# Six of eight value tiles of the second mixer as Strassen-Winograd pairs, with two weight sums made by adding transfers

## The reference

```python
h = rmsnorm(x, p["mix_norm"][layer])
proj = h @ p["w_in_c"][j]
u = proj[..., :D_C]
v = layernorm(proj[..., D_C:], ...)
z = spatial_gating(v, p["sgu_w"][j], p["sgu_bias"][j])
x = x + (u * z) @ p["w_out_c"][j]
```

## Time and profile before

| | |
|---|---|
| median of 3 runs | 1179.95 us |
| lowest, highest | 1179.23, 1180.22 us |
| span of the profiled execution | 1178.1 us |
| TensorE busy | 1166.1 us |
| last output products, first ConvFFN | 541 to 580 us |
| value units | 580 to 632 us |
| U units, with turning and gating of V | 632 to 705 us |

### The profile page before, as it was taken

How to read it: one execution, slowest core, us unless ns; L and a number is a source line. 1 busy time by engine, 2 the same in 40 slices (tenths; PEclk the granted TensorE clock), 3 DMA queues, 4 the chain that set the end, 5 groups by cost and what they waited for, 6 DMA issues and landing times. The chain is left out here.

```text
span 1178.1 us, 21481 instructions
## 1 busy us (share of the span) xinstructions
PE 1166.1 (99%) x8562; PEld 1146.4 (97%) x8562; DVE 738.1 (63%) x1358; ACT 523.9 (44%) x929; POOL 646.5 (55%) x647
## 2 busy tenths in 40 slices
PE   8999999999999999999999999999999999999997
PEld 8887999999999999999999999999999999999997
DVE  5999766578655786545414644455776557864554
ACT  7465554444344453334412533354443444434452
POOL 3986353448934489343464323345488454884433
PEclk9999999999999999999999999999999999999999
DMA  6310342221422214213322222322124222242212
GB/s 229 115 63 28 76 154 88 71 72 57 145 87 72 71 49 152 87 54 98 119 74 88 68 68 88 110 72 88 55 72 144 72 83 61 72 144 72 67 55 82
DMA packets 33365, 103.74 MB, mean 88 GB/s; under 512 B 4849, under 2 KB 6897, under 8 KB 33265
## 3 DMA queue, kind: packets, MB, share of 16 engines
q1 hardware_dynamic: 29200, 98.92, 25.6%
q10 hardware_dynamic: 4080, 3.69, 1.0%
HBM read 98.29 MB, written 4.79 MB: 87 GB/s over the span
## 5 line engine op out<-in xcount | busy, mean ns | idle before, releaser
L443 PE MATMUL psum<-x_hi,w_hi 128*128 128x288 f32 x1820 | 392.3, 297 | 1.3 <-POOL w_lo L1404 1.3
L443 PE MATMUL psum<-x_hi,w_lo 128*128 128x288 f32 x1820 | 389.8, 296 | 0.0
L443 PE MATMUL psum<-x_lo,w_hi 128*128 128x288 f32 x1820 | 389.7, 296 | 0.0
L1404 POOL TENSOR_TENSOR w_lo<-w_raw,w_hi 128x1024 fp32r<-128x1024 f32 (+2 forms) x100 | 222.5, 2228 | 227.2 <-ACT w_hi L860 227.2
L443 PEld LDWEIGHTS psum<-x_hi,w_hi 128*128 128x128 f32 x1820 | 293.4, 189 | 3.6 <-POOL w_lo L1404 1.6
L443 PEld LDWEIGHTS psum<-x_hi,w_lo 128*128 128x128 f32 x1820 | 293.2, 189 | 0.0
L443 PEld LDWEIGHTS psum<-x_lo,w_hi 128*128 128x128 f32 x1820 | 293.2, 189 | 0.0
L2070 DVE SCALAR_TENSOR_TENSOR psum<-arena,params,psum 128x608 f32<-128x608 f32 x176 | 150.6, 856 | 88.2 <-ACT psum L1205 83.9
L1404 POOL TENSOR_TENSOR w_lo<-arena,w_hi 128x1024 fp32r<-128x1024 f32 (+1 forms) x49 | 114.5, 2337 | 119.5 <-ACT w_hi L860 119.5
L690 PE MATMUL psum<-block_hi,w_hi 128*128 128x288 f32 x448 | 133.6, 298 | 0.0
L690 PE MATMUL psum<-block_hi,w_lo 128*128 128x288 f32 x448 | 133.2, 297 | 0.0
(11 more groups left out here) (232 smaller groups left out, 1666.8 us busy)
## 6 DMA issues: line engine op xcount, KB each, us to landing
w_raw<-in_w_up SPq DMA_DIRECT2D x44, 512.0 KB, 3.3
arena<-in_w_up SPq DMA_DIRECT2D x44, 512.0 KB, 3.2
w_raw<-in_w_down SPq DMA_DIRECT2D x16, 512.0 KB, 3.6
arena<-in_w_down SPq DMA_DIRECT2D x16, 512.0 KB, 3.7
w_raw<-in_w_in_c SPq DMA_DIRECT2D x16, 512.0 KB, 3.2
w_raw<-in_w_in_ab SPq DMA_DIRECT2D x11, 512.0 KB, 3.4
w_raw<-in_w_out_ab SPq DMA_DIRECT2D x16, 256.0 KB, 2.6
w_raw<-in_w_out_c SPq DMA_DIRECT2D x8, 512.0 KB, 3.3
```

What stands on the lines that cost most here:

```text
L443: last = nc.tensor.matmul(PS[:, 2 * (q % 2 if slot is None else slot) + half, 0:HALF], w[q][:, k * P:(k + 1) * P], r[:, r_at, half * HALF: ...
L1404: nc.gpsimd.tensor_tensor(w_lo[slot][:, 0:nk * P], raws[RAW_SLOT[RAW[u]]][:, 0:nk * P], w_hi[slot][:, 0:nk * P].bitcast(F32), ALU.subtract ...
```

## The change

Value tiles 2 to 7 are computed as three pairs. With x cut into two halves of channels and two halves of tokens, and the weights of a pair into two halves of input channels by two output tiles, a pair is a 2x2 product of blocks, and seven products of blocks (4 input tiles x 3 terms = 12 matmuls each) take the place of eight. For this

- VectorE and ScalarE make four sums of blocks of x, split into high and low parts (`x_sums`, `x_sums_hi`), inside the loop over the last output tiles of the first ConvFFN, whose tiles now come in the order 0, 4, 1, 5, 2, 6, 3, 7;
- two of the four sums of weights of a pair (R3, S1) are made by transfers: SP loads A21 twice into a buffer, then a transfer issued by GpSimd adds A11 and A22 to them; VectorE makes the other two (S2, R4);
- each weight block is split on its own (ScalarE, GpSimd, 512 columns), up to eight ahead;
- products accumulate in PSUM on top of copies of earlier ones, which ScalarE makes (`bank_copy`), and VectorE combines the rest on evacuation (`take_c11` to `take_c21`);
- VectorE adds up V in place of GpSimd;
- w_in_c tiles use all four raw buffers; the hidden values of the last group, `xh` and `xl` and two output buffers lie elsewhere, and the scratch for GpSimd's transfers is made smaller to have room.

```diff
+    PAIR_ORDER = ("A11", "S1", "S2", "A12", "R3", "R4", "A22")
+    PAIR_BANK = [{"A11": a, "A12": a, "S1": a + 1, "S2": 0, "R4": 0, "R3": 1, "A22": 1} for a in (2, 6, 2, 6)]
+    PRODUCT_HALF = [(4 + n) % 8 for n in range(N_PRODUCTS - 1)] + [4]
...
+                    raw_tile(m % 4, U_PAIR[m // 2] + (PLACE["A22"] if m % 2 else PLACE["R4"]) + 1)
...
+        X_SUMS_AFTER = (2, 3, 5, 7)
...
+                        if m in (3, 5, 7):
+                            if m > 3:
+                                sp.wait_ge(unit_done, U_IN1)
+                            for n in range(2):
+                                sp.dma_start(dma_sums_of(m // 2)[:, n, :], w_in_c[m, :, 0:KL2]).then_inc(ld_a21[m // 2 - 1], 16)
...
+            unit(0, U_IN1, KD, xh, xl, xl_ready, KD * 2, order=SPLIT_ORDER)
+            def second_norm_sums():
+                pe.wait_ge(xt_ready, 4 * (KD // 2))
+                wide_sums(2)
+
+            unit(1, U_IN1 + 1, KD, xh, xl, middle=second_norm_sums, at_tile=2)
...
+                for n, name in enumerate(PAIR_ORDER):
+                    pe.wait_ge(lo_ready, base + n + 1)
+                    if name == "A11" and p > 1:
+                        pe.wait_ge(acc_free, U_PAIR[p - 2] + 2 if p > 2 else U_IN1 + 2)
+                    elif name == "S2":
+                        pe.wait_ge(pair_copy, copies + 1)
+                    elif name == "R3":
+                        pe.wait_ge(pair_copy, copies + 3)
+                    elif name == "A22":
+                        pe.wait_ge(pair_copy, copies + 4)
...
+            def x_sums_hi(k):
+
+                if k:
+                    act.wait_ge(xt_ready, 4 * k)
+                else:
+                    act.wait_ge(h_lo_ready, H_FFN[0] + NT)
+                nc.scalar.activation(PS[:, M0, 0:HALF], X[:, k, HALF:T], ACT.Identity, bias=0.0,
+                                     scale=pcol("mix_norm", KD + k)).then_inc(xt_hi, 1)
+                for block, bank, sign, made in ((X1, M1, 1.0, 1), (X3, S0, 1.0, 3), (X2, S1, -1.0, 4), (X4, M0, -1.0, 4)):
+                    act.wait_ge(xt_sum, 4 * k + made)
+                    nc.scalar.activation(xth[:, block, k, :], PS[:, bank, 0:HALF], ACT.Copy, scale=sign).then_inc(xt_hi, 1)
...
+            for n in range(1, 4):
+                product_weight_hi(n)
             wide_roots(3)
+            for n in range(4, 8):
+                product_weight_hi(n)
+            for n in range(N_PRODUCTS):
+                if PAIR_ORDER[n % 7] in ("A11", "S1", "S2", "R3"):
+                    bank_copy(n // 7 + 1, PAIR_ORDER[n % 7])
+                if n + 8 < N_PRODUCTS - 1:
+                    product_weight_hi(n + 8)
+                if n == N_PRODUCTS - 5:
+                    product_weight_hi(N_PRODUCTS - 1)
+                    split_n(U_U, U_IN1 + 2 + 14)
+                    split_n(U_U + 1, U_IN1 + 2 + 16)
...
+            def dma_sums(p):
+
+                pool.wait_ge(ld_a21[p - 1], 32)
+                nc.gpsimd.dma_start(dma_sums_of(p), lower_and_upper(p), accum_op=ALU.add).then_inc(dma_sum[p - 1], 16)
+
+            dma_sums(1)
+            for n in range(N_PRODUCTS):
+                product_weight_lo(n)
+                if n in (2, 8):
+                    dma_sums(2 if n == 2 else 3)
...
+            def x_sums(k):
...
+                stt(out=t1, in0=x11, scalar=low, in1=b12, op0=ALU.mult, op1=ALU.subtract).then_inc(xt_sum, 1)
+                stt(out=t3, in0=x22, scalar=high, in1=b12, op0=ALU.mult, op1=ALU.subtract).then_inc(xt_sum, 1)
+                dve.wait_ge(xt_sum, 4 * k + 2)
+                stt(out=t2, in0=x11, scalar=low, in1=t3, op0=ALU.mult, op1=ALU.add).then_inc(xt_sum, 1)
+                dve.wait_ge(xt_sum, 4 * k + 3)
+                stt(out=t4, in0=x21, scalar=high, in1=t2, op0=ALU.mult, op1=ALU.subtract).then_inc(xt_sum, 1)
+                for a, (block, src, sign) in enumerate(((X1, t1, 1.0), (X3, t3, 1.0), (X2, t2, -1.0), (X4, t4, -1.0))):
+                    dve.wait_ge(xt_hi, 5 * k + a + 2)
+                    stt(out=xtl[:, block, k, :], in0=src, scalar=sign, in1=xth[:, block, k, :].bitcast(F32),
+                        op0=ALU.mult, op1=ALU.subtract).then_inc(xt_ready, 1)
...
+            for kind in PAIR_SUMS:
+                pair_weight_sum(1, kind)
             dve.wait_ge(st_ffn, 16)
             wide_factors(3)
-            for m in range(KD):
-                scaled(U_IN1 + m, V[:, m, :])
-            uu = U_IN1 + KD
+            scaled(U_IN1, V[:, 0, :])
+            scaled(U_IN1 + 1, V[:, 1, :])
+            add_v(1)
+            for p in range(1, V_PAIRS):
+                if p < V_PAIRS - 1:
+                    pair_weight_sum(p + 1, "S2")
+                take_c11(p)
+                take_c22(p)
+                if p < V_PAIRS - 1:
+                    pair_weight_sum(p + 1, "R4")
+                take_c12(p)
+                add_v(2 * p)
+                take_c21(p)
+                add_v(2 * p + 1)
...
+    nc = bacc.Bacc("TRN2", target_bir_lowering=False, num_devices=1, dynamic_dma_scratch_size=8192)
```

More of the change, by code:

```diff
@@ L95, in hybrid_trunk @@
     U_IN1 = U_FFN0 + N_FFN
-    U_OUT1 = U_IN1 + 2 * KD
+    V_PAIRS = KD // 2
+    U_PAIR = [None] + [U_IN1 + 2 + 7 * n for n in range(V_PAIRS - 1)]
+    N_PRODUCTS = 7 * (V_PAIRS - 1)
+    U_U = U_IN1 + 2 + N_PRODUCTS + 1
+    U_OUT1 = U_U + KD
     U_FFN1 = U_OUT1 + KD
@@ L135, in hybrid_trunk @@
         IN0[u] = g
-    assert KH == 4 and not any(u % 4 for u in (U_OUT0, U_FFN0, U_IN1, U_OUT1, U_FFN1, *U_GROUP))
+    assert KH == 4 and not any(u % 4 for u in (U_OUT0, U_FFN0, U_IN1, U_OUT1, U_FFN1, U_U, *U_GROUP))
     def tiles_of(u):
@@ L416, in _ @@
                     for m in range(KD):
-                        load(r0 + 2 * n + m, w_down[layer, m, :, t0 * P:(t0 + n) * P])
+                        tile = SPLIT_ORDER[m] if layer == 0 and t0 + n == KF else m
+                        load(r0 + 2 * n + m, w_down[layer, tile, :, t0 * P:(t0 + n) * P])
             for n, r in enumerate(LAST[0][1]):
@@ L1626, in ffn @@
                         continue
-                    for m in range(3, KD + (0 if layer else 3)):
+                    for m in range(3, KD + (0 if layer else 2)):
                         if layer == 0:
@@ L2119, in ffn @@
                         continue
-                    for m in range(KD):
-                        residual(ud + m, m, 2 if m == 2 else None)
-                        x_lo(2, m, "mix_norm", KD + m)
+                    for m, tile in enumerate(SPLIT_ORDER):
+                        residual(ud + m, tile, 2 if m == 2 else None)
+                        x_lo(2, m, "mix_norm", KD + tile, tile)
                         if m:
                             add_square(2, m)
+                        if m in X_SUMS_AFTER:
+                            x_sums(X_SUMS_AFTER.index(m))
             def last_stage(ud):
@@ new lines, in add_v @@
+            def add_v(m):
+                v_acc = PS[:, S0:S1 + 1, 0:HALF]
+                if m < 2:
+                    dve.wait_ge(acc_free, U_IN1 + 2)
+                else:
+                    dve.wait_ge(acc_free, U_PAIR[m // 2] + (7 if m % 2 else 3))
+                    dve.wait_ge(vsum, m - 1)
+                nc.vector.tensor_tensor(halves(sq[:, 0, :]) if m == KD - 1 else v_acc, halves(V[:, 0, :]) if m == 1 else v_acc,
+                                        halves(V[:, m, :]), ALU.add).then_inc(vsum, 1)
@@ L2191, in u_take @@
+            uu = U_U
             def u_take(m):
-                scaled(uu + m, U[:, m, :])
+                scaled(uu + m, U[:, m, :], U_SLOT[m])
+            U_SLOT = (1, M0 // 2, *(m % 2 for m in range(2, KD)))
             def v_norm(m):
```

238 lines of the change are left out of this document (172 added, 66 removed).

## The result

The changed kernel takes 1186.79 us (median of 4 runs, 1186.61 to 1187.00) against 1179.81 before on the same chip; the ratio is 1.006, its 95% interval 1.0046 to 1.0073. The prediction was 1181.2 with a range of 1176.5 to 1186.0, so it is outside by 0.8 us. The profiled spans are 1184.6 and 1178.1, 6.5 apart.

What follows compares the result with a forecast made beforehand. TensorE's instruction count was taken as the bound: 4.80 us removed, waits of 1.6, 0.4, 0.7, 0.9, 1.6 and 0.8 added, +1.2 on the 1178.1 span, 1179.3; with 1.85 for the runs' median, 1181.2; range 1176.5 to 1186.0.

Steps and rivals of the forecast that it cites:

- Removed work: Value tiles 2 to 7: 288 matmuls become 252; 36 fewer at 0.1333 save 4.80 us, all on the path.
- A: Last output tiles: input sums delay tile 5's residual add, so the seventh output product waits 1.6 us.
- B: First value tile: the third group of sums delays tile 7's add; TensorE waits 0.4 us.
- C: Second value tile: TensorE waits 0.7 us for banks that the last group of input sums uses.
- D: Pair 1: weight sums before the reciprocals delay the first product's copy; the third product waits 0.9 us.
- E: Pair 1: ScalarE splits the next weight sum before copying the third product; the fifth product waits 1.6 us.
- F: Pair 2: the third adding transfer lands at 614.1, delaying weight sum, split and copy; the fifth product waits 0.8 us.
- Splits, loads, moved buffers: Pairs: GpSimd's weight splits stay ahead of TensorE, SP's six loads are hidden, moved buffers cost nothing.
- transfers late: Slower rival, pairs 1 and 2: adding transfers land late, +2.5 at 7.6 us, +6.0 at 9.8 (1186.0); chance 0.25.
- GpSimd the bound: Slower rival, pairs 2 and 3: splits at 1.75 make TensorE wait 2.9 us in place of F, 1183.3; chance 0.1.
- VectorE and GpSimd not meeting: Faster rival: only the encounter at 554 to 558 remains, A 1.4, B to E nothing, 1176.9; chance 0.2.

Runs made afterwards that it cites:

- the last version: Changed kernel with two adding transfers issued earlier, the third behind product 11's split, both selects behind the third U split, S2's copy before the weight-sum split: 1183.26 us.
- the filled run: Changed kernel with 24 useless matmuls ahead of TensorE's wait for the fifth product of pair 1: 1186.37 us.
- the paused run: Changed kernel with GpSimd waiting, before its two affine selects, for VectorE's add of the first two value tiles and next weight sum: 1192.51 us.
- the pair with one select each: Changed kernel with plain loads, one select moved behind the third U split: 1181.96 us with the 128-partition select left in the stretch, 1184.45 with the 64-partition one.
- the last two kernels: Changed kernel with four steps moved, third adding transfer issued ahead of three splits: 1184.90 us; the same with that issue behind product 11's split: 1183.26 us.
- the add from PSUM: Changed kernel with the first value tile also written, scaled, to PSUM, so VectorE's first add of V has one SBUF input: 1187.09 us.
- the copy first: Changed kernel with ScalarE copying the third product of pair 1 before it splits pair 2's weight sum: 1188.55 us.

## Why the prediction was wrong

- **Removed work:** right. 252 matmuls, 0.133 apart outside the half-clock stretches.
- **A:** right, 1.62 for 1.6, behind VectorE's residual.
- **B:** 0.31 for 0.4. The profile names no releaser.
- **C:** the place was wrong and the size too small. The wait is for the last input tile (1.76). Half of it comes from the squares add at 584.48, which is held 2.73 by a split that follows the issue of the first adding transfer; with the issue moved it took 1.83 and the wait was 0.9. I had costed this issue only by its length. The wait for the sums that I named is hidden by the half-clock stretch at 590: it comes out, 0.6, in every kernel with the sums in this order that has no such stretch, also where the tile is still 1.8 late.
- **D:** nothing for 0.9. The copy (601.25) is there when the third product can start.
- **E:** this is the step that failed most. Its chain (weight sum, split, copy, fifth product) is what the trace shows. Its size was not: I gave the add 1.9, one late end of 0.6 behind the running GpSimd operation, and it took 6.77. The wait is 3.72, not 1.6. The sum priced the issues by their length and the two selects at nothing; what they do to a VectorE operation with two SBUF inputs was no term of it.
- **F:** nothing for 0.8, though the landing (5.6 us, below) was near the 6.4 assumed. The fifth product of pair 2 starts at 622.45, 6.4 us later than in my walk, while the third transfer, issued at 611.44 instead of 607.7, lands 2.9 later, so it has 3.5 more. When the pairs were put back in time, in the last version, the wait of 1.5 came.
- **The clock:** not in the prediction. Two stretches of 3.4 us at 0.50 cost 1.5 each by their matmuls. I had taken a wait for its length alone, on the evidence of a kernel whose waits of 1.2 us leave the clock at 1.00. Of the net loss it was less: the first stretch hides the 0.6 for the sums, and filling the second wait gave nothing clear.
- **Splits, loads, moved buffers:** nothing, as costed. SP's six loads of 256 KB land in 5.0, not 3.2; GpSimd waits 4.1 for the third pair's, where I had 1.5, but TensorE for none.
- **Rivals:** transfers late: no, 5.6 us. GpSimd the bound: not in the changed kernel, but it is next in line, as the 1.1 in the filled run and the paused run show. VectorE and GpSimd not meeting: not in this kernel. Without the input sums the time is near its 1176.9 (1177.8), but by chance, since they meet there too, 4 us twice.

The terms: 6.0 assumed for A to F; measured 7.4 of waits, 3.0 of half clock, 0.9 of what the idle figures leave out and late starts, and 0.2 of rest: 11.5. The miss would have been 1.7 larger if D and F had come as forecast; that they were nothing is luck, since the delay of E gave F its room. The range missed since its upper end came from the landing alone, with the hold of the add kept at its forecast value.

What is shown: the hold needs two SBUF inputs (0.77 against 4.5 to 6.8), and a GpSimd stretch that holds an issue or the 64-partition select (the pair with one select each, the old kernel with a select and with an issue in the same place, and the last two kernels, 5.19 against 0.92, which differ in the place of one issue). What stays open: by what means, and why it ends only when GpSimd pauses; and how much each of the issue and the select adds in the changed kernel, where both are there.

## What to carry over

A VectorE operation with two SBUF inputs, beside GpSimd's operations without a gap, is cheap only while these are uniform: keep issues of transfers and operations over fewer partitions out of such a stretch, or take one input from PSUM, and then look at the next operation with two (it was held instead, and nothing was gained). Price a wait of TensorE by what the clock does behind it, and look for the wait that the slow stretch covers. And extra work for an engine that feeds TensorE in order (here 3.3 us of sums, four times) was not placed away here: TensorE waited 3.7 us in one order and 3.8 in the other, and without it the kernel was some 9 us faster.

## What the runs showed of the hardware

- VectorE's 128x576 add of two SBUF tiles: 0.77 us alone, 1.73 to 1.93 beside GpSimd's splits, 3.79 with a 64-partition select among them, 4.79 with both selects, 6.77 with an issue too. The last three end 0.6 behind GpSimd's next pause, so their length is the distance to that pause and no price of the select or the issue.
- Behind an issue of 1.20 us (512 KB) GpSimd's splits of 128x512 are 1.70 long and start 1.24 apart, each 0.45 before the last has ended; without one, and behind one of 0.55 us (16 KB), they are some 1.3 long at the same 1.24.
- The two groups in the changed kernel's list of transfers that answer to the open prices, then the plain transfer of GpSimd's in the old kernel with an issue:

```profile
arena<-in_w_in_c SPq DMA_DIRECT2D x6, 256.0 KB, 5.0
arena<-in_w_in_c POOLq DMA_DIRECT2D x3, 512.0 KB, 5.6
```

```profile
spare<-in_w_down POOLq DMA_DIRECT2D x4, 16.0 KB, 3.9
```

- So a transfer that GpSimd issues and that adds to SBUF lands in 5.6 us (6.5 in the kernel without input sums), 1.7 times the plain 3.3 of SP's of its size. How much of that is the adding stays open, as no plain one of 512 KB was issued by GpSimd; but its plain one of 16 KB took 3.9 already. The estimate of 3.2 by the Trainium skill's page "DMA: Bandwidth & Descriptors" (section "Anatomy of one DMA — SWDGE (gpsimd) path") is too little for the one that adds, and the same formula, an estimate of 2.0 for 16 KB, for the small plain one.
- TensorE's clock fell to 0.50 behind every wait of 2.2 us and more; behind a wait of 1.76 to 1.79 it fell in the changed kernel and stayed at 1.00 in four others (the add from PSUM, GpSimd paused, the copy first, the wait filled); behind 1.74 (the copy first) and behind 1.62, 1.5, 1.4 and 1.2 it stayed. A stretch at 0.50 is 3.4 us long or 6.8, and 3.4 of it cost 1.5 us of matmuls. What else decides is open.
